# Low-rank gate of a gated linear attention layer: from a padded three-part product to raw fp32 tiles in four column tiles, with the first keys' product beside the loading

## What is computed

```python
u = _rmsnorm(h, ln1_g[i])
proj = u @ w_in[i]
q, k, v, g, g_lr, cb, cc, cx = jnp.split(proj, offsets, axis=-1)      # g_lr has 16 columns
gate_logits = (g_lr @ w_gate_up[i] + b_gate[i]).astype(jnp.float32)  # 16 -> 256
log_a = jax.nn.log_sigmoid(gate_logits) / GATE_NORMALIZER
...
o = _gla_chunked(qh, kh, vh, ah)     # needs q, k, v and log_a
...
bias = rel_bias.astype(jnp.float32)[t5_bucket(rel)]   # second block, used much later
```

## Time and profile before

| | us |
|---|---|
| median of 3 runs | 1674.89 |
| lowest, highest | 1674.39, 1675.41 |
| span of the profiled execution (first to last instruction) | 1673.8 |
| busy in it: PE, DVE, POOL, ACT | 1628.5, 1150.5, 710.5, 623.2 |
| mean granted clock of PE | 0.996 |

### The profile page before, as it was taken

How to read it: one execution, slowest core, us unless ns; L and a number is a source line. 1 busy time by engine, 2 the same in 40 slices (tenths; PEclk the granted TensorE clock), 3 DMA queues, 4 the chain that set the end, 5 groups by cost and what they waited for, 6 DMA issues and landing times.

```text
span 1673.8 us, 21585 instructions
## 1 busy us (share of the span) xinstructions
PE 1628.5 (97%) x7862; PEld 1331.6 (80%) x7862; DVE 1150.5 (69%) x1702; ACT 623.2 (37%) x980; POOL 710.5 (42%) x390
## 2 busy tenths in 40 slices
PE   9999999999999999999999999999989999999997
PEld 6888787888877888888887778887858888878775
DVE  7231799972498777777767756886965993497456
ACT  6041334421164444444443222264561112268214
POOL 2443211145515233332326687753465555442552
PEclk9999999999999999999999999999999999999999
DMA  5511010123423444334459986331101111110012
GB/s 194 86 39 51 25 39 26 39 72 142 162 114 116 178 159 151 139 143 160 154 184 348 401 336 251 114 142 60 51 13 51 50 41 49 56 45 1 27 37 101
DMA packets 54455, 190.27 MB, mean 114 GB/s; under 512 B 5793, under 2 KB 7730, under 8 KB 53722
## 3 DMA queue, kind: packets, MB, share of 16 engines
q1 hardware_dynamic: 49250, 171.61, 28.3%
q10 hardware_dynamic: 5112, 17.44, 3.6%
HBM read 133.97 MB, written 55.05 MB: 113 GB/s over the span
## 4 chain that ended last, share of the span: by engine, by line
PE 52%; DVE 7%; DMA 3%; issue 2%; POOL 2%; SPq 1%; ACT 1%; ACTq 0%; POOLq 0%; DVEq 0%
PE G L788 16%; PE U L1035 10%; PE G L1035 10%; PE U L1073 4%; PE G L1073 4%; PE G L1109 2%; PE U L1279 1%; SPq L504 1%; PE G L1268 1%; DMA hid_spill<-hst 1%; DMA raw<-in_weights 1%; DMA fraw<-in_weights 1%; PE G L1192 1%; DVE h L2342 1%; DMA hid_spill<-hst_last 1%
## 5 line engine op out<-in xcount | busy, mean ns | idle before, releaser
L611 POOL TENSOR_SCALAR w_hi<-raw 128x1024 fp32r<-128x1024 f32 x50 | 149.4, 2988 | 286.1 <-PE G L788 214.2
L788 PE MATMUL G<-B_hi,w_hi 128*128 128x512 f32 x512 | 159.7, 393 | 3.3 <-DVE B_lo L1963 2.4
L788 PE MATMUL G<-B_lo,w_hi 128*128 128x512 f32 x512 | 157.7, 389 | 0.0
L788 PE MATMUL G<-B_hi,w_lo 128*128 128x512 f32 x512 | 157.6, 389 | 0.0
L788 PE MATMUL G<-A_hi,w_hi 128*128 128x512 f32 x448 | 144.3, 403 | 0.3 <-DVE w_lo L1976 0.3
L654 POOL TENSOR_TENSOR S<-fraw 128x512 f32<-128x512 f32 x33 | 47.2, 1430 | 222.0 <-DVE ring_lo L2237 195.1
L788 PE MATMUL G<-A_lo,w_hi 128*128 128x512 f32 x448 | 139.3, 392 | 0.0
L788 PE MATMUL G<-A_hi,w_lo 128*128 128x512 f32 x448 | 138.6, 391 | 0.0
L613 POOL TENSOR_TENSOR w_lo<-raw,w_hi 128x1024 fp32r<-128x1024 f32 x50 | 132.8, 2655 | 4.2
L1035 PE MATMUL G<-X_lo,ring_hi 128*128 128x512 f32 x308 | 120.3, 391 | 2.2 <-DVE X_lo L2232 2.2
L1035 PE MATMUL G<-X_hi,ring_hi 128*128 128x512 f32 x308 | 120.1, 390 | 1.7 <-DVE ring_lo L2237 1.2
(11 more groups left out here) (395 smaller groups left out, 3788.8 us busy)
## 6 DMA issues: line engine op xcount, KB each, us to landing
raw<-in_weights SPq DMA_DIRECT2D x72, 512.0 KB, 3.6
hid_spill<-hst SPq DMA_DIRECT2D x72, 512.0 KB, 2.6
fraw<-in_weights SPq DMA_DIRECT2D x66, 512.0 KB, 4.5
Dc<-hid_spill SPq DMA_DIRECT2D x56, 512.0 KB, 12.9
Dc<-hid_spill ACTq DMA_DIRECT2D x14, 512.0 KB, 8.0
h<-in_x_t SPq DMA_DIRECT2D x8, 512.0 KB, 7.8
h_spill<-h SPq DMA_DIRECT2D x8, 512.0 KB, 6.7
pj_spill<-pj_out SPq DMA_DIRECT2D x8, 512.0 KB, 2.9
```

The costliest lines, as they stand in the source:

```text
L611: pool.tensor_scalar(hi, raw[:, u, :], 1.0, None, ALU.mult).then_inc(w_hi_done, 1)
L788: mm = pe.matmul(G[g][:, b * HT:(b + 1) * HT], w, x[:, k, b * HT:(b + 1) * HT], start=s0, stop=s1)
```

## The change

The gate's 16 columns are no longer taken from a padded slot in three parts. DVE multiplies them with the norm's gains into a small tile `lr`, in which each tile of 128 features has 16 zero columns, the 16 weights and 16 zero columns. PE multiplies the raw fp32 tiles of `h` by 32 columns of it. Tile k goes to the PSUM partitions 32j to 32j+31 with j = k mod 4, so that four partial results stand under each other in `G[0]`; this is done in two calls of 8 matmuls. `wgu` is 128 rows high now, with the gate's weights repeated for each of the four partial results, so that the next product adds them up. The window of 32 columns of `lr` is chosen so (`c = RANK if j else 0`) that the 16 results stand at partitions 16 to 31 for j = 0 and at the first 16 of their 32 partitions for the others; the rest is zero. Partition 0 of `glT`, free in this way, is set to one, and row 0 of `wgu` holds the bias b_gate.

The first keys' product takes the gate's place beside the loading and writes to `G[1]`; the gate's two calls stand inside it. `first_sums` moves with the rest: it stands before tile 1 of the third slot's product now. The slots' indices 0 and 1 change places in `raw`, `w_hi` and `w_lo`; POOL splits from slot 3 on, ACT and DVE split slots 1 and 2.

```diff
@@ SP @@
             for k in range(KT):
+                if k == 4:
+                    load(0, 0)
                 sp.dma_start(h[:, k, :], x_t[:, k * T:(k + 1) * T]).then_inc(tile_in[k], 16)
-            load(1, 1)
+            sp.wait_ge(w_split, 2)
+            load(0, 2), load(1, 3)
...
+            sp.wait_ge(ones_done, 2)
+            sp.dma_start(wgu[0:1, :], w_gate_up[RANK:RANK + 1, :]).then_inc(const_in, 16)
+            for j in range(4):
+                at_row = 32 * j + (0 if j else RANK)
+                sp.dma_start(wgu[at_row:at_row + RANK, :], w_gate_up[0:RANK, :]).then_inc(const_in, 16)
@@ POOL @@
+            split(1, S_KQ + 2, bufs[1])
+            with pool.Fori(1, (S_CONV - 1) // 2) as i:
@@ PE @@
+            def low_rank(half):
+
+                if half == 0:
+                    pe.wait_ge(w_split, 2)
+                for b in range(2):
+                    for j in range(4):
+                        k = 4 * half + j
+                        if b == 0:
+                            pe.wait_ge(tile_in[k], 16)
+                        c = RANK if j else 0
+                        mm = pe.matmul(G[0][32 * j:32 * j + 32, b * HT:(b + 1) * HT], lr[:, k, c:c + 32], h[:, k, b * HT:(b + 1) * HT],
+                                       start=(half == 0), stop=(half == 1))
+                if half:
+                    mm.then_inc(acc_done, 1)
+
             for k in range(KT):
+                if k in (5, 7):
+                    low_rank(k // 2 - 2)
...
-            gemm(1, S_KQ, None, 1, A_hi, A_lo, free=False)
-            gemm(0, S_KQ + 1, 1, 0, A_hi, A_lo, before={4: first_sums})
-            gemm(1, S_KQ + 2, 1, 1, A_hi, A_lo)
+            gemm(0, S_KQ + 1, 1, 0, A_hi, A_lo)
+            gemm(1, S_KQ + 2, 1, 1, A_hi, A_lo, before={1: first_sums})
...
-                mm = pe.matmul(U[:, c // 2, c % 2 * 256:c % 2 * 256 + 256], glT[0:RANK + 1, c * P:(c + 1) * P], wgu[:, :],
+                mm = pe.matmul(U[:, c // 2, c % 2 * 256:c % 2 * 256 + 256], glT[:, c * P:(c + 1) * P], wgu[:, :],
@@ ACT @@
-            first_hi(1)
+            first_hi(2)
             for k in range(KT):
                 squares(h[:, k, :], k % 2, max(k - 1, 0))
-                if k == 2:
-                    act.wait_ge(ones_done, 2)
+                if k == 1:
                     act.wait_ge(acc_done, 1)
-                    act.activation(glT[0:RANK, :], G[0][0:RANK, :], ACT.Copy).then_inc(acc_free[0], 1)
+                    act.activation(glT[:, :], G[0][:, :], ACT.Copy).then_inc(acc_free[0], 1)
+                if k == 4:
+                    act.wait_ge(acc_done, 2)
+                    act.activation(kT[:, 0, :], G[1][:, :], ACT.Copy).then_inc(acc_free[1], 1)
@@ DVE @@
+            def low_rank_weights():
+
+                dve.wait_ge(w_in[0], 16)
+                gains = vecs[:, VEC["ln1"]:VEC["ln1"] + KT].unsqueeze(2).broadcast_to([P, KT, RANK])
+                dve.tensor_tensor(lr[:, :, RANK:2 * RANK], raw[:, 0, :].rearrange("p (k n) -> p k n", k=KT)[:, :, 0:RANK],
+                                  gains, ALU.mult).then_inc(w_split, 1)
...
-            first_low(1)
+                if k == 3:
+                    low_rank_weights()
+            first_low(2)
...
-            dve.tensor_tensor(glT[0:RANK, :], glT[0:RANK, :], R[0:RANK, :], ALU.mult).then_inc(low_done, 1)
+            tick(dve.tensor_tensor(glT[:, :], glT[:, :], R[:, :], ALU.mult))
+            tick.wait()
+            dve.memset(glT[0:1, :], 1.0).then_inc(low_done, 1)
```

More of the change, by code:

```diff
@@ L50 @@
 ATT_TICKS = 6
-CONSTS = 9
+CONSTS = 13
 S_GATE = 0
@@ L211, in build @@
         tri = at("tri", C0 + 2, [P, P])
-        wgu = at("wgu", C0 + 2.5, [RANK + 1, GLA_H * DK])
+        wgu = at("wgu", C0 + 2.5, [P, GLA_H * DK])
+        lr = at("lr", 120, [P, KT, 3 * RANK])
         lmask = at("lmask", C0 + 3.5, [P, LEVELS, P // 2], I32)
@@ L468, in _ @@
             for k in range(KT):
+                if k == 4:
+                    load(0, 0)
                 sp.dma_start(h[:, k, :], x_t[:, k * T:(k + 1) * T]).then_inc(tile_in[k], 16)
-            load(1, 1)
+            sp.wait_ge(w_split, 2)
+            load(0, 2), load(1, 3)
             small = [(ones, consts[:, P:2 * P]), (oneh, onehot), (relb, rel_bias), (win, window), (ident, consts[:, 0:P]),
-                     (tri, consts[:, 2 * P:3 * P]), (wgu, w_gate_up)]
+                     (tri, consts[:, 2 * P:3 * P])]
             for dst, src in small:
                 sp.dma_start(dst[:, :], src).then_inc(const_in, 16)
+            sp.wait_ge(ones_done, 2)
[3 more added lines that the diff above has]
+                sp.dma_start(wgu[at_row:at_row + RANK, :], w_gate_up[0:RANK, :]).then_inc(const_in, 16)
             sp.dma_start(lmask[:, :, :], masks[:, 0:LEVELS * P // 2].rearrange("p (l n) -> p l n", l=LEVELS)).then_inc(const_in, 16)
             sp.dma_start(dmask[:, :], masks[:, LEVELS * P // 2:]).then_inc(const_in, 16)
-            assert len(small) + 2 == CONSTS
-            with sp.Fori(0, (S_PROJ - 3) // 2) as i:
+            assert len(small) + 7 == CONSTS
+            with sp.Fori(1, (S_PROJ - 3) // 2) as i:
                 for u in range(2):
@@ L854, in _ @@
                     for b in range(2):
-                        mm = pe.matmul(G[0][:, b * HT:(b + 1) * HT], w, x[:, k, b * HT:(b + 1) * HT], start=(k == 0 and e == 0),
+                        mm = pe.matmul(G[1][:, b * HT:(b + 1) * HT], w, x[:, k, b * HT:(b + 1) * HT], start=(k == 0 and e == 0),
                                        stop=(k == KT - 1 and e == 2))
+                        if k == 0 and e == 0 and b == 0:
+                            mm.then_inc(w_used, 1)
             mm.then_inc(acc_done, 1)
@@ L1367, in squares @@
                 act.activation(sq[:, u, :], src, ACT.Square, scale=scale).then_inc(sq_done, 1)
-            act.dma_start(raw[:, 0, :], weights[0]).then_inc(w_in[0], 16)
+            act.dma_start(raw[:, 1, :], weights[S_KQ]).then_inc(w_in[1], 16)
             act.wait_ge(ones_done, 1)
@@ L1373, in _, with first_hi @@
             tick.wait()
-            def first_hi(u):
-                act.wait_ge(w_in[u], 16)
+            def first_hi(s):
+                u = s % 2
+                act.wait_ge(w_in[u], s * 8 + (16 if u == 0 else 8))
                 act.activation(w_hi[:, u, :], raw[:, u, :], ACT.Copy).then_inc(w_hi_done, 1)
-            first_hi(0)
+            first_hi(1)
             act.wait_ge(vec_in, 16)
@@ L1397, in _ @@
             root(1, U01, 1.0 / D, "eps", at_stat=1)
-            act.wait_ge(acc_done, 2)
-            act.activation(kT[:, 0, :], G[1][:, :], ACT.Copy).then_inc(acc_free[1], 1)
+            act.wait_ge(acc_done, 3)
+            act.activation(kT[:, 1, :], G[0][:, :], ACT.Copy).then_inc(acc_free[0], 1)
             act.wait_ge(fv_done, 1)
@@ L1970, in _, with first_low @@
             dve.wait_ge(ones_done, 1)
-            dve.memset(glT[0:RANK + 1, :], 1.0).then_inc(ones_done, 1)
-            def first_low(u):
-                dve.wait_ge(w_hi_done, u + 1)
-                dve.tensor_tensor(w_lo[:, u, :], raw[:, u, :], f(w_hi[:, u, :]), ALU.subtract).then_inc(w_split, 1)
-            first_low(0)
+            dve.memset(wgu[:, :], 0.0).then_inc(ones_done, 1)
+            dve.memset(lr[:, :, :], 0.0).then_inc(w_hi_done, 1)
+            def first_low(s):
+                u = s % 2
+                dve.wait_ge(w_hi_done, s + 1)
+                dve.tensor_tensor(w_lo[:, u, :], raw[:, u, :], f(w_hi[:, u, :]), ALU.subtract).then_inc(w_split, 1)
+            def low_rank_weights():
[3 more added lines that the diff above has]
+                                  gains, ALU.mult).then_inc(w_split, 1)
+            first_low(1)
             dve.wait_ge(vec_in, 16)
```

8 lines of the change are left out of this document (4 added, 4 removed).

## The result

| | before | after |
|---|---|---|
| median, first comparison, 10 runs each | 1674.89 | 1679.29 |
| lowest, highest | 1674.39, 1676.2 | 1676.75, 1680.6 |
| ratio, 95% interval | | 1.0022 [1.0014, 1.003] |
| ratio in a second comparison (11 and 27 runs) | | 1.0016 [1.0007, 1.0025] |
| span of the profiled execution | 1673.8 | 1674.7 |

By its ratio the first comparison gives +3.7 us (0.0022 of 1674.89), or 1678.6; the second +2.7. The kernel got slower by a little more than can be told from no change.

What follows compares the result with a forecast made beforehand. Two equally long paths to 93.9 us, PE's products and the bias write's chain to `la`, were taken to bound the beginning. Terms -0.1 and +1.9 gave +1.8, so 1674.89 became 1676.7; range 1673.9 to 1679.0.

Steps and rivals of the forecast that it cites:

- Part 1: Loading stage up to `first_sums`: it starts at 35.8, 0.3 us earlier than before, with PE's products 7.2 us ahead.
- Part 2: Path from root and bias write to `la`: ready at 93.8 against 93.9; term -0.1 us, between -0.5 and +0.4.
- the shift gets through: Bias write lands before PE's logits, so PE's 7.2 us count in full: 1667.7; chance 5%.
- Part 3: PE after `first_sums`: 138 matmuls instead of 168, then 9.2 us idle waiting for `la` until 93.8.
- Part 4: Behind PE's wait for `la`: PE starts the cumulative sums at half clock, losing 1.9 us, ends 0 and 3.4.
- +1.9: Clock term behind PE's wait for `la`: half of a 3.3 to 4.2 us half-rate stretch lost, 1.7 to 2.1 us.

Runs made afterwards that it cites:

- e6: Changed kernel with the gate's 16 matmuls all in the first column tile, one after the other; 1688.57 us, ratio 1.0079 to the kernel before.
- e9: Kernel before, unaltered, one execution for a second trace; 1675.72 us, span 1673.9.
- e3: Kernel before with fvec moved and ACT not waiting for the bias write ahead of the log_a chain; 1673.75 us, ratio 0.9996.
- e7: Kernel before without ACT's bias-write wait ahead of log_a, and with 128 rows instead of 17 in the logits' product; 1673.48 us, ratio 0.9985.
- e2: Changed kernel with fvec moved and ACT not waiting for the bias write ahead of the log_a chain; 1667.59 us, ratio 0.9957 to the kernel before.
- e4: Changed kernel with table product and bias write moved earlier, ACT's wait left in place; 1666.56 us, ratio 0.9952 to the kernel before.
- e1: Changed kernel with slot 6's first 36 matmuls made twice to fill PE's wait; 1675.72 us, ratio 1.0000 to the kernel before.
- e8: Changed kernel with 18 matmuls of slot 6 made twice, so PE still waits 5.17 us; 1677.75 us, ratio 1.0014 to the kernel before.

## Why the prediction was right, and where it was short

**The beginning (Part 1).** The times came out within 0.35 us at each step, but partly by luck, since an early start made up for half of what two terms lacked. PE's first product began at 7.15 and not at 7.49; in the traces of this study the start lies between 7.01 and 7.49, and the trace the prediction was made from had the latest. Tile 4 was taken up at 13.48 (13.6 predicted), but its late `A_hi` and `A_lo` cost 0.86 where 0.4 was put: from the start of the product to the first call it is 8.32 us (7.15 to 15.47), and the same five tiles took 7.46 before (7.49 to 14.95). The two calls cost 1.85 each (1.95), and the slower first matmuls behind them and the way into the second another 0.36, so 4.1 together and not 3.9. Slot 2's product began at 23.63 (23.3), `first_sums` at 35.98 and its sums at 36.94 (35.8, 36.7). The squares were ready at 35.45 (22.26 plus 13.19), a cover of 1.5 us where 0.8 was expected. That four column tiles run beside each other was read from one row of another stage and is shown by `e6`. The estimate from the Trainium skill's 2.38 for three tiles (TensorE: Matmul & The Clock Gate, Part 3: Packing small matmuls) was 4.3 us for both calls; they took 3.7 from start to next row, 4.1 with what followed. So the estimate from the page and the 3.9 from the trace were each off by 0.2.

**The second path (Part 2).** Right. Issue at 38.97 (38.8), ACT's first step at 83.10 (83.0), the sums at 93.89 (93.8). Only that `first_sums` would come 0.3 earlier than before does not hold beyond the first trace: the write is issued between 38.85 and 39.18 in the four traces of the changed kernel, and between 38.41 and 38.65 in `e9`, `e3` and `e7`, which have the old order. With the 39.09 of the first trace taken in, the means still differ by 0.4 us, the other way. `e2` and `e4` show that the write held back the changed kernel: with its landing off the path, or its issue 9.9 us earlier, 7.2 and 8.0 us come through. The rival "the shift gets through" failed only on the write.

**PE's wait (Part 3).** Right: 9.30 us, 9.2 predicted, but without a reason for one part of it. The sum takes slot 6 at full clock (73.6 to 84.6), although have the half rate in that place; and "the logits' product has the same columns and 128 instead of 17 rows: no term" missed that the half clock behind this product goes away with the rows. `e7` puts it at 2.1 us of PE. In the changed kernel it had no effect on the time because it only lengthened a wait.

**The clock (Part 4).** The mechanism was right, and `e1` shows it alone: fill the wait, and the loss behind it is gone. The step that was short is the term itself, "+1.9". The four traces have 1.5, 1.6, 2.6 and 2.7 behind the wait, 2.1 in the mean. On top of it comes 1.5 near 181 us in two of the four, 0.75 in the mean. The sum is 2.9 in place of 1.9, and the two ratios say 3.7 and 2.7. (The spans of the profiled executions say 2.6: 1676.5 in the mean of four, 1673.85 of two.) The median measured, 1679.29, is just above the range's 1679.0; the ratio's 1678.6 is inside it. The argument for +1.9 took the length of the half-rate stretch from other places, 3.3 to 4.2 us, and halved it, as if the whole of it lay behind PE's return. In all four traces it was 10.2 us long and began within the idle time, near 87 or near 89, so that 3.2, 3.4, 5.5 and 5.7 us of it lay behind the return. About half of that is what was lost (1.5, 1.6, 2.6, 2.7). That 1.9 lies between these values is not owed to the argument. The statement that the half rate behind the 17 rows "costs nothing of note before" holds in the trace it was read from and not in `e9`, where PE came 1.2 us behind `la`.

**The rule.** The Trainium skill (TensorE: Matmul & The Clock Gate, Part 1: The HAM clock gate) has it that gaps between bursts of matmuls bring the half rate back. The traces agree: 0.50 from 87 on in the wait of 9.30 us, 1.00 from 93 to 99 in `e1`, whose wait is 1.10. They also show what this sentence doesn't cover: in the kernel before, the half rate came back while PE was busy without a gap, behind the 17 rows.

**What stays open.** Whether the half clock near 181 us belongs to the change. It is there in two of four traces of it and in none of two of the kernel before (nor in `e3` and `e7`, built on that kernel), but it is also in `e1`, where the first wait and its loss are gone. Both times in the unaltered kernel it came with the larger loss behind the wait. Of the other kernels built on the changed one, `e4` has it (169.7 to 173.1, in a timeline that is 9 us ahead there) and `e2` and `e6` have not. So the count when `e9` was planned was four of seven traces with the change, not four of six. So few traces don't tell a cause from a coincidence. Besides, the stage from about 893 to 1130 us takes between 236.1 and 238.1 us in these traces with the same instructions, 237.5 in that of before and 236.5 in the first of after; this is part of why the first trace has a span only 0.9 above that of before.

## What to carry to other kernels

Before a product is made shorter, look for the other chain that ends at PE's next wait, even if that wait is 0.4 us: two paths of equal length hide one another, and taking 7 us off one of them gave none back here. Here the cure was to issue a 42 us write, whose data was nearly ready, ten microseconds earlier: the change alone cost 0.2%, with this it gains 0.5%. Where a wait can't be removed, its price in a kernel that is bound by PE was not zero but the clock behind it, and a wait of 5 us (`e8`) cost what one of 9 us did.

## What the runs showed of the hardware that was not expected

- The granted clock fell to half while PE was busy without a gap, behind or within 16 records of 17 rows (0.76 in the mean over 79 to 86 us in `e3`; also in `before`, and for 6.8 us in `e9`), and stayed at 1.00 behind the same records with 128 rows, in `e7` and in every trace of the changed kernel.
- With a wait of the same length in the same program (8.9 to 9.3 us) the half rate lasted 10.2 us in each of four executions, but began near 87 or near 89 us, and the time lost behind the wait was 1.5 and 1.6 or 2.6 and 2.7 us. One trace shows only one of the two. In `e6`, with a wait of 8.87 us, the half rate lasted 6.8 us (99.8 to 106.6) and cost 1.3.
- Four column tiles of 32 columns with fp32 operands ran 3.8 times as fast as one (6.98 to 1.85 us for 8 matmuls of 512 columns, from their start to the next row).
- The broadcast write of 2.10 MB from 8 partitions kept its pace with different weight loads beside it: from issue to ACT's start 44.0 us before, 44.1 after, 43.7 in `e6`.
